# Expert gates by accumulating indirect DMAs into DRAM cells, in place of one-hot products

## What is computed

```python
s = jnp.einsum('thpd,hpnd->thpn', q, keys)            # 8 heads, 2 halves, 128 keys each
top_s, top_i = lax.top_k(s, PEER_TOPK)                 # 16 of 128 per half
cand = top_s[:, :, 0, :, None] + top_s[:, :, 1, None, :]
best_s, best_j = lax.top_k(cand.reshape(..., 256), PEER_TOPK)
expert = i1 * PEER_KEYS + i2                           # one of 16384 experts
g = jax.nn.softmax(best_s, axis=-1)
act = gelu(einsum('thkd,td->thk', u[expert], xc)) * g
out = einsum('thk,thkd->td', act, v[expert])
```

## Time and profile before

| what | value |
|---|---|
| time, three runs | 2735.97, 2736.47, 2739.0 us (median 2736.47) |
| the profiled execution: its time | 2744.57 us |
| the profiled execution: its span | 2742.8 us |
| PE busy | 2465.3 us (90%) |
| DVE busy | 2131.3 us (78%) |
| ACT busy | 1234.8 us (45%) |
| POOL busy | 571.3 us (21%) |
| DMA, mean | 254 GB/s, 697.60 MB |

### The profile page before, as it was taken

The page is one execution under the profiler, slowest core; times in us unless marked ns, Lnnn a source line. Parts: engine busy times, 40 slices in busy tenths (PEclk is TensorE's granted clock), DMA queues, the critical chain, the costliest instruction groups (busy, mean ns, idle before and its releaser), DMA issues.

```text
span 2742.8 us, 36197 instructions
## 1 busy us (share of the span) xinstructions
PE 2465.3 (90%) x10956; PEld 1938.4 (71%) x10956; DVE 2131.3 (78%) x3891; ACT 1234.8 (45%) x2704; POOL 571.3 (21%) x408
## 2 busy tenths in 40 slices
PE   4987888999899787899999999998878999999996
PEld 3767766666456576777777777776756888878885
DVE  4877613666388855889999999989688888888888
ACT  2332043444312142267777787777433333333333
POOL 2013104422032320011111111112122323232221
PEclk9999999999999899999999999999988999999998
DMA  6646651112032325478888888888899999999996
GB/s 275 217 163 253 255 218 62 62 62 86 23 117 101 146 78 217 136 263 309 322 299 319 298 319 309 305 304 313 318 387 347 381 382 388 384 368 380 389 382 237
DMA packets 223810, 697.60 MB, mean 254 GB/s; under 512 B 15840, under 2 KB 111456, under 8 KB 181472
## 3 DMA queue, kind: packets, MB, share of 16 engines
q1 hardware_dynamic: 165984, 367.25, 37.2%
q0 software_dynamic: 37632, 270.55, 26.0%
q10 hardware_dynamic: 20096, 58.72, 5.6%
HBM read 614.67 MB, written 81.79 MB: 254 GB/s over the span
## 4 chain that ended last, share of the span: by engine, by line
PE 42%; DVE 32%; DVEq 9%; DMA 8%; issue 5%; ACT 3%; SPq 1%; ACTq 1%; POOL 0%; PEldq 0%; PEld 0%
PE ps L866 21%; PE ps L557 7%; DVE g_acc L1787 5%; DVEq L1799 4%; PE ps L542 4%; DVE rows L1778 4%; DVE arena L1454 3%; DMA act_in<-act_scratch 3%; DVE hot L1741 2%; PE ps L569 2%; DMA arena<-in_weights 2%; DVE cand L1397 1%; PE ps L905 1%; DMA rows<-in_rows,pick_e 1%; DMA ring<-in_weights 1%
## 5 line engine op out<-in xcount | busy, mean ns | idle before, releaser
L1999 POOL DMA_INDIRECT rows<-in_rows,pick_e x256 | 333.4, 1302 | 1350.1 <-DVE g_acc L1787 1188.6
L1245 ACT CAST t_hi<-raw 128x1024 fp32r<-128x1024 f32 x256 | 268.8, 1050 | 545.0 <-PE ps L866 528.1
L866 PE MATMUL ps<-t_hi,c_hi 128*128 128x512 f32 x1024 | 407.4, 398 | 37.9 <-DVE t_lo L1859 33.0
L866 PE MATMUL ps<-n_hi,t_hi 128*128 128x512 f32 x1024 | 413.6, 404 | 26.4 <-DVE t_lo L1804 25.3
L866 PE MATMUL ps<-t_lo,c_hi 128*128 128x512 f32 x1024 | 404.4, 395 | 0.0
L866 PE MATMUL ps<-t_hi,c_lo 128*128 128x512 f32 x1024 | 404.1, 395 | 0.0
L866 PE MATMUL ps<-n_hi,t_lo 128*128 128x512 f32 x1024 | 401.2, 392 | 0.0
L866 PE MATMUL ps<-n_lo,t_hi 128*128 128x512 f32 x1024 | 401.0, 392 | 0.0
L1787 DVE SCALAR_TENSOR_TENSOR g_acc<-rows,small,g_acc 128x1024 f32<-128x1024 f32 x254 | 326.3, 1285 | 34.9 <-issue 9.1
L1934 POOL TENSOR_TENSOR w_lo<-ring,w_hi 128x1024 fp32r<-128x1024 f32 x76 | 189.4, 2498 | 667.2 <-ACT w_hi L998 559.9
L866 PEld LDWEIGHTS ps<-t_hi,c_hi 128*128 128x128 f32 x1024 | 196.2, 192 | 85.3 <-issue 44.5
(11 more groups left out here) (198 smaller groups left out, 4188.4 us busy)
## 6 DMA issues: line engine op xcount, KB each, us to landing
raw<-in_table SPq DMA_DIRECT2D x256, 512.0 KB, 7.2
ring<-in_weights SPq DMA_DIRECT2D x44, 2048.0 KB, 8.2
act_scratch<-act_out SPq DMA_DIRECT2D x128, 256.0 KB, 3.5
gate_scratch<-staged ACTq DMA_DIRECT2D x16, 2048.0 KB, 9.7
act_in<-act_scratch SPq DMA_DIRECT2D x128, 256.0 KB, 10.6
gate_in<-gate_scratch SPq DMA_DIRECT2D x32, 1024.0 KB, 15.6
arena<-in_weights ACTq DMA_DIRECT2D x24, 1024.0 KB, 9.4
arena<-in_weights SPq DMA_DIRECT2D x2, 2048.0 KB, 21.2
```

What stands on the lines that cost most here:

```text
L866: last = mm(out, a, b_, start=start and x == 0, stop=stop and x == len(pairs) - 1, skip_group_check=True)
L1245: copy(t_hi[:, t % 2, :], raw[:, t % 4, :]).then_inc(hi_ready, 1)
L1999: G.indirect_dma_start(rows[:, j % 4, :], None, rows_in, bass.IndirectOffsetOnAxis(ap=pick_e[:, j:j + 1], axis=0)).then_inc(row_in[j % 4], 16)
```

## The change

The one-hot products are gone, with their buffers, the transposes, the staging and its stores. In their place stands an array of 16384 x 512 single-element *cells* in DRAM (33.5 MB), a row of 512 tokens for each expert.

- During the second trunk SP writes zeros to all cells: 32 DMAs of 1 MB (`clear`), four after the third weight load, then two after each further one up to the z phase; the source is one half of `score_in`, cleared by POOL at the program's start.
- The 32 searches are now taken head by head (two blocks of tokens of the same head make a *pair*). They stand half a search per tile in tiles 0 to 15 and a quarter per tile in tiles 16 to 111. After a pair DVE works out each result's cell number (`place_pair`), ACT the exponentials (`exp_pair`), DVE the gates (`weigh_pair`).
- For each of the 32 x 16 result columns POOL issues one indirect DMA that adds 128 gates (4 bytes each, one token per partition) into 128 cells (`scatter`, 512 of them). They stand behind the gathers on POOL, 4 or 5 per tile. Sixteen of them wait until the sixteen before them for the same tokens have landed.
- After its last store of activations SP waits until all scatters have landed, then loads the gates of tile 0 to 3; `load_gate` loads 256 KB for one tile in runs of 2 KB.
- Slots: one per tile in tiles 16 to 127, then one per tile with a second in every eighth tile. AHEAD is 3. The combine pass is written out on DVE and ACT instead of a loop.

```diff
-        gate_dram = scratch("gate_scratch", QUARTERS, P, P, STAGE)
+        gate_cells = scratch("gate_scratch", P * P * SEQS[1], 1)
+        gate_dram = gate_cells.rearrange("(k p t) a -> k p (t a)", p=P, t=SEQS[1])
+        gate_zero = gate_cells.rearrange("(c p m n) a -> c p m (n a)", c=ZEROS, p=P, n=2 * P)
...
         def slots_of(k):
+            if k < DENSE:
+                return ()
+            if k < P:
+                return (k - DENSE,)
+            j = k - DENSE + (k - P + 4) // 8
+            return (j, j + 1) if k % 8 == 3 else (j,)
...
+                def clear(c):
+                    sp.dma_start(gate_zero[c], score_in[:, 1].rearrange("p a n -> p (a n)").unsqueeze(1).broadcast_to(
+                        (P, P * P * SEQS[1] // (ZEROS * P * 2 * P), 2 * P))).then_inc(zeroed, 16)
...
+            def load_gate(i, t):
+                after(sp, coef_ready, 4 * i + (t - 3))
+                sp.dma_start(gate_in[:, t, :], gate_dram[bass.ds(4 * i + t, 1)].rearrange("a p n -> (a p) n")
+                             ).then_inc(gate_loaded[t], 16)
...
             store_act(P - 1)
+            for x in range(4):
+                sp.wait_ge(scattered[x], 16 * TOPK * HEADS)
+            for t in range(4):
+                load_gate(0, t)
...
-            for stage in range(1, 4):
-                turn_block(stage)
-                c = SEARCH_BODIES + 8 * (stage - 1)
-                for t in range(4):
-                    score(4 * c + t, t)
-                    gate_step(32 * (stage - 1) + t, t % 2, stage)
...
+            with pe.Fori(1, P // 4) as i:
                 for t in range(4):
                     score(4 * i + t, t)
...
+            def place_pair(p):
+                o, n, b = 32 * (p % 2), 32 * p, 2 * (p % 2)
+                keys1, keys2, v = (sel[:, x, o:o + 32] for x in range(3))
+                stt(out=keys1, in0=keys2, scalar=float(P), in1=keys1, op0=ALU.mult, op1=ALU.add)
...
+                for x in range(2):
+                    ts(cell[:, n + TOPK * x:n + TOPK * (x + 1)], keys1[:, TOPK * x:TOPK * (x + 1)], float(SEQS[1]),
+                       token[:, b + x:b + x + 1], ALU.mult, ALU.add)
...
+            def scatter(s):
+                b = s // TOPK % 4
+                if s % (2 * TOPK) == 0:
+                    pool.wait_ge(pair_ready, s // (2 * TOPK) + 1)
+                if s % TOPK == 0:
+                    after(pool, scattered[b], 16 * TOPK * (s // (4 * TOPK)))
+                G.indirect_dma_start(gate_cells, bass.IndirectOffsetOnAxis(ap=cell[:, s:s + 1], axis=0),
+                                     cell_g[:, s:s + 1], None, compute_op=ALU.add).then_inc(scattered[b], 16)
...
+            sent = 0
             for k in range(2 * P):
                 for j in slots_of(k):
                     if j + AHEAD < SLOTS:
                         gather(j + AHEAD)
+                known = 2 * TOPK * sum(pair_of(x) is not None for x in range(min(k, P)))
+                pace = 5 if k < DENSE or k % 4 == 0 else 4
+                while sent < known and (pace > 0 or k == P - 1):
+                    scatter(sent)
+                    sent += 1
+                    pace -= 1
```

More of the change, by code:

```diff
@@ L375, in load @@
                     load_unit(weights[UNITS_ADA + n], (b + n) % 2)
+                    if g and n == 2:
+                        sp.wait_ge(zero_ready, 1)
+                        for c in range(4):
+                            clear(c)
+                    if g and n in (9, 10):
+                        for c in range(2 * n - 2, 2 * n):
+                            clear(c)
                 if g == 0:
@@ L390, in _ @@
                         load_unit(weight_unit(2 * i + (UNITS_ADA + 9 + j)), (b + 9 + j) % 2)
+                        if g:
+                            for x in range(2):
+                                clear(4 * i + (2 * j + x + 16))
                 load(17, z_done, 8 * g + 7)
@@ L463, in _ @@
                 load_tile(k + 4)
[L464 to L473 removed]
+                for x in range(2, SEARCHES):
+                    if starts(x - 1) == k:
+                        load_scores(sp, False, x)
                 if k == P // 2:
@@ L1807, in _ @@
             for k in range(P):
-                i, t = k // 4, k % 4
-                block = (i + 1 - SEARCH_BODIES) // 8 + 2 if (i + 1 - SEARCH_BODIES) % 8 == 0 else None
-                if block is not None and t == 0:
-                    shift_block(block % 2, 1)
-                for s in steps_of(k):
-                    hot_keys(s)
                 lower_tile(k + 1)
@@ L1818, in _ @@
                     use_slot(j)
+                if k and pair_of(k - 1) is not None:
+                    weigh_pair(pair_of(k - 1))
                 m, parts = search_of(k)
                 for part in parts:
[L1821 to L1827 removed]
+                    search(False, m, 16 * (m % 4), part)
+                if pair_of(k) is not None:
+                    place_pair(pair_of(k))
+            coefficient(0, 0)
+            coefficient(0, 1)
             split_coef(0, 0)
@@ L1844, in finish_gathered, with turn @@
                 tt(y, y, f_x1a[:, x, :], ALU.add).then_inc(y_ready, 1)
-            def turn(i, t, half, static=None, last=False):
-                if static is not None:
-                    slots = slots_of(static)
-                    use_slot(slots[0])
-                else:
-                    dve.wait_ge(row_in[t], 16 * i + 16 * (P // 4 + 1))
-                    V.tensor_tensor_reduce(out=rows[:, t, 0:D], in0=rows[:, t, 0:D], in1=x_tok[:, 1, :], scale=1.0,
-                                           scalar=0.0, op0=ALU.mult, op1=ALU.add, accum_out=dot[:, t:t + 1]
-                                           ).then_inc(dotted, 1)
+            def turn(i, t, last=False):
+                slots = slots_of(P + 4 * i + t)
+                use_slot(slots[0])
                 if not (last and t == 3):
```

284 lines of the change are left out of this document (75 added, 209 removed).

## The result

The changed kernel takes 3064.05 us (median of four runs, 3062.86 to 3076.86), against 2737.36 for the kernel before (four runs, 2735.97 to 2739.0) on the same chip: **a ratio of 1.1204, 95% interval 1.1173 to 1.1234.** The forecast was 2765 with a range to 3010; slower was right, the size was not. The profiled execution has a span of 3061.6 us.

What follows compares the result with a forecast made beforehand. POOL's scatter issues were taken to bound the score pass: +48 there, +5 turn, -26 combine pass, +2 second trunk, together +29, so 2773.6 us with the profiler and 2765 as median; range 2640 to 3010.

Steps and rivals of the forecast that it cites:

- the price of the scatter: POOL in the score pass: a scatter's issue taken as the gather's 0.94 us plus 0.10, 1.04 us.
- The sum: Score pass: POOL's 512 scatters (763 us) and 107 gathers (149 us), 912 us from 1080, last scatter leaving at 1992.
- The range: Whole kernel: 2640 to 3010 us, leaving out POOL costing nothing and every scatter at the dearest.
- The reason for 0.10: Scatter's issue on POOL: an add must fetch the cell as well as the gate, so 0.10 us over a gather.
- The wait: POOL's DMA issue waits for a running DVE instruction with two tensor inputs: 0.15 us per issue taken.
- the gap of 0.30: POOL: 0.30 us between two DMAs in a row, added to each scatter and gather.
- DVE's own sum: Score pass if nothing else were late: DVE's list and PE-paced last tiles give 828 us, 85 less than 913.
- Rival 1: Score pass: POOL is no bound, kernel faster; 2713 us at the gather's issue price, 2632 without wait; chance 0.31.
- the turning point: Score pass: mean POOL issue at which the rest's gain is used up, 883 us for 619 issues, 1.43 us each.
- Rival 2: Score pass: tiny reads and writes fill POOL's queue and hold POOL; pass +299, total +280, 3016 us; chance 0.26.
- Combine pass: Last pass: between 694 us at PE's 5.42 a tile and the old 750, the middle 724 taken: -26 us.
- Trunk and turn: Second trunk: 32 clears behind weight loads, +2 us; turn between passes: first gates loaded after last activation store, +5 us.

Runs made afterwards that it cites:

- The write: The changed kernel with its 512 scatters as plain indirect writes, without the add: 2771.59 us, ratio 1.0119 to the kernel before.
- the fetch: The changed kernel with each scatter replaced by an indirect gather of 128 cells into a spare buffer: 2766.6 us, ratio 1.0108 to the kernel before.
- the late add: The changed kernel with the row add at the end of a combine tile instead of behind the row dot: 3052.59 us, ratio 1.1144 to the kernel before.

## Why the prediction was wrong

**The step that failed** is the price of the scatter: "An add must fetch the cell as well as the gate, so I take 0.10 more, 1.04." It measured 1.55 as a floor, 0.51 us more, and 512 x 0.51 is 261 us. The mechanism around it held: POOL is the bound, issues back to back, DVE waits for rows and PE for DVE's split. The sum ran from 1080 over 912 us to 1992; the last scatter left at 2264.2 after a start at 1087.4. Of the difference of 272, 7 are the later start, 253 the scatters (860.0 + 155.8 where 763 stood) and the rest the gathers among them. The range failed with it. Its upper end cut off the case in which "every scatter is at the dearest", 1.68: that was the mean. Of the whole difference of 319 us between the two profiled executions, 313 are the score pass.

**The reason for 0.10** was wrong, too. The write, the fetch and the row gather issue at one price, so fetching alone costs nothing at the issue; the indexed add has a price of its own, 0.58 us. The nearest row was the nearest in shape, not in operation, and no row of the trace held an accumulating DMA.

**The wait** for two-input DVE instructions was taken as 0.15 and measured 0.13; the gap of 0.30 held to the hundredth.

**DVE's own sum** of 828 us stands against 809 without scatters. *Rival 1* was right that POOL's mean issue decides. At the write's price the 619 issues took 890 us (1084.7 to 1974.8), 1.44 each, where the prediction put the turning point at 1.43; the kernel was 1.2% slower there, mainly because the combine pass gave back 5 us (749.0 to 744.5) in place of 26. The Trainium skill, DMA: Bandwidth & Descriptors, "Anatomy of one DMA — SWDGE (gpsimd) path", calls descriptor generation small. By the prediction's reading of it the cell's fetch adds nothing to the issue, and the indirect write and fetch agree, which issue at the gather's price; the add does not, with 0.58 us more from the first DMA on.

*Rival 2* gave 3016, near the result, by another mechanism: a full queue. The first scatters already cost 1.55, the queues' share fell to 0.71 and rows landed in 5.7 us, so it was the issue. That its price, 1.68 + 0.30, is just the mean that came is luck: the 1.68 was a gather that waited for DVE. The prediction's sign for it, a mean above 1.5 us, does not tell a full queue from a dear add; the landing time does.

*PE's clock* was granted at 0.82 in the stretch from 1600 to 1800, and PE still waited there for DVE's split, so the clock did not set the pass.

**Combine pass:** -26 was forecast (724 us), -5 came (744.3). Two terms were missing or too small. The row add's new place behind the dot, which the prediction did not speak of, cost 14 us (744.3 to 730.5 by the late add). The second slots cost 32 (730.5 to 698.5), where the prediction had only taken the middle of its bounds. The lower bound itself, 694 us at PE's pace, was sound: the pass with single slots reached 698.5.

**Trunk and turn:** +2 and +5 were forecast; the pass starts 3.8 us later and the turn takes 6 us more.

## What to carry to other kernels

Before work is moved to an idle engine, multiply its count by a price measured for that very operation: 512 small DMAs at 2 us each are a millisecond, however few bytes they carry. If no row shows the operation, the range has to reach past the dearest neighbour, not stop short of it. And where engines run in step, tile by tile, a tile with double work can stop them each time, even where the mean would fit: here PE lost 1.2 to 1.6 us at each second slot, though DVE's list of 4.9 + 2.5 / 8 = 5.2 us a tile is under PE's 5.45.

## What the runs showed of the hardware that I had not expected

- An accumulating indirect DMA of 128 cells takes POOL 1.55 us to issue where a writing or fetching one takes 0.95 to 0.98; with 64 cells it is 1.42. One that began 0.13 us or more inside a two-input DVE instruction ended 1.42 to 1.45 us after it.
- Direct accumulating DMAs of 128 cells overlap on POOL, 0.92 us of its time each, and filled the queues (share 1.08, rows landing after 22.1 us); the indirect ones, spaced 1.98 us apart, did not (0.71, 5.7 us).
- A DMA share of 1.0 did not by itself mean a bound: PE ran at its own pace beside 1.01, and loading only a quarter of the gates' bytes left it at 0.98.
